# Adding the experts' rows to a running sum in DRAM, instead of keeping them and gathering them at the end

## What is computed

```python
scores = jax.nn.sigmoid(t @ w_router)                    # 512 tokens x 64 experts
# group-limited choice of 8 experts for each token, then
w = w / jnp.sum(w, -1, keepdims=True) * ROUTED_SCALE     # the token's 8 gates
h = silu(einsum('td,edf->tef', xb, w_gate)) * einsum('td,edf->tef', xb, w_up)
routed = einsum('tef,efd->td', h * gb[:, :, None], w_down)
shared = (silu(t @ ws_gate) * (t @ ws_up)) @ ws_down
x = layernorm(ALPHA * x + (1.0 + g2) * (routed + shared), ln2_g, ln2_b)
```

## Time and profile before

| | |
|---|---|
| median of 3 runs | 1363.83 us (1359.28 to 4515.15) |
| profiled execution: its time | 1363.99 us |
| its span, first to last instruction | 1362.2 us |
| mean granted clock of TensorE, share of full speed | 0.927 |
| PE, PEld, DVE, ACT, POOL busy | 87%, 66%, 56%, 26%, 11% |
| DMA read and written | 310.56 MB and 40.39 MB |

### The profile page before, as it was taken

How to read it: one execution, slowest core, us unless ns; L and a number is a source line. 1 busy time by engine, 2 the same in 40 slices (tenths; PEclk the granted TensorE clock), 3 DMA queues, 4 the chain that set the end, 5 groups by cost and what they waited for, 6 DMA issues and landing times.

```text
span 1362.2 us, 16041 instructions
## 1 busy us (share of the span) xinstructions
PE 1186.4 (87%) x5690; PEld 899.2 (66%) x5690; DVE 760.9 (56%) x1179; ACT 352.7 (26%) x533; POOL 149.2 (11%) x135
## 2 busy tenths in 40 slices
PE   2889997996989988779999999999999999999400
PEld 2443444655644577668888888888888888888300
DVE  4565698755224753665555555555555555555398
ACT  0222312225640021222222322222222222222100
POOL 0000000000000000440000000000000010000276
PEclk9787998997999999789999999999999999999755
DMA  9994253006100344569999999999999999995293
GB/s 352 327 338 160 78 81 104 1 4 231 75 1 16 123 171 156 211 228 325 362 352 356 349 355 352 352 350 351 360 344 356 352 355 349 358 354 206 94 374 134
DMA packets 77528, 333.56 MB, mean 245 GB/s; under 512 B 14601, under 2 KB 16521, under 8 KB 52537
## 3 DMA queue, kind: packets, MB, share of 16 engines
q1 hardware_dynamic: 58104, 291.05, 58.7%
q0 software_dynamic: 14112, 33.58, 6.8%
q10 hardware_dynamic: 5280, 8.53, 1.9%
HBM read 310.56 MB, written 40.39 MB: 258 GB/s over the span
## 4 chain that ended last, share of the span: by engine, by line
PE 72%; DVE 15%; DMA 7%; ACT 2%; issue 2%; SPq 2%; POOL 0%; ACTq 0%; POOLq 0%; DVEq 0%
PE ps L632 31%; PE ps L655 14%; PE ps L684 5%; PE ps L1481 4%; PE ps L1271 4%; DVE acc L922 3%; DMA xg<-u_rows,idx 3%; PE ps L1279 3%; DMA fk<-in_w_ada 3%; DVE big L1595 2%; PE ps L1345 2%; DVE small L1593 2%; DVE big L1527 2%; SPq L959 2%; PE ps L1451 1%
## 5 line engine op out<-in xcount | busy, mean ns | idle before, releaser
L632 PE MATMUL ps<-wx,xT 128*128 128x256 f32 x2048 | 452.8, 379 | 1.7 <-DVE xT L876 1.0
L632 PEld LDWEIGHTS ps<-wx,xT 128*128 128x128 f32 x2048 | 384.7, 190 | 51.6 <-issue 2.0
L751 DVE TENSOR_TENSOR wd_lo<-wx,wd_hi 128x2048 fp32r<-128x2048 f32 x65 | 149.0, 2292 | 40.8 <-ACT wd_hi L558 38.7
L558 ACT ACTIVATE wd_hi<-wx 128x2048 fp32r<-128x2048 f32 x64 | 122.3, 1911 | 143.5 <-PE ps L655 143.5
L504 POOL DMA_INDIRECT xg<-u_rows,idx x66 | 65.6, 994 | 667.3 <-DVE idx L867 667.0
L884 DVE TENSOR_TENSOR yrow<-ps,vg 128x512 f32<-128x512 f32 x64 | 44.3, 692 | 147.7 <-PE ps L655 147.7
L655 PE MATMUL ps<-wd_hi,hT_hi 128*128 128x512 f32 x272 | 116.5, 428 | 10.9 <-DVE hT_lo L756 9.5
L1271 PE MATMUL ps<-uT,ring 128*128 128x512 f32 x272 | 120.5, 603 | 0.0
L567 ACT ACTIVATE hs<-ps 128x256 f32<-128x256 f32 x68 | 26.1, 384 | 333.3 <-PE ps L632 333.3
L655 PE MATMUL ps<-wd_hi,hT_lo 128*128 128x512 f32 x272 | 111.6, 410 | 0.0
L745 DVE TENSOR_TENSOR hs<-hs,ps 128x256 f32<-128x256 f32 x68 | 28.6, 420 | 147.6 <-ACT hs L567 147.6
(11 more groups left out here) (268 smaller groups left out, 1376.3 us busy)
## 6 DMA issues: line engine op xcount, KB each, us to landing
wx<-in_w_gate SPq DMA_DIRECT2D x64, 1024.0 KB
wx<-in_w_up SPq DMA_DIRECT2D x64, 1024.0 KB
wx<-in_w_down SPq DMA_DIRECT2D x64, 1024.0 KB
expert_rows<-yrow SPq DMA_DIRECT2D x64, 512.0 KB
ring<-in_w_in SPq DMA_DIRECT2D x6, 2048.0 KB, 16.0
vg<-in_w_ada SPq DMA_DIRECT2D x4, 2048.0 KB, 9.1
fk<-in_w_ada SPq DMA_DIRECT2D x4, 2048.0 KB, 10.4
ring<-in_w_ada SPq DMA_DIRECT2D x3, 2048.0 KB, 13.7
```

The lines of the kernel that those rows point to most:

```text
L558: act.activation(wd_hi[:], flat_weights(s)[2], ACT.Copy).then_inc(wd_hi_ready, 1)
L632: mm = pe.matmul(ps[u % 2][:, k * ED:(k + 1) * ED], lhs(j), w[:, j, :], start=(j == 0), stop=(j == KD - 1))
L751: dve.tensor_tensor(wd_lo[s][:], w, wd_hi[:].bitcast(F32), ALU.subtract).then_inc(wd_ready, 1)
```

## The change

The gate is applied to an expert's row when the row leaves PSUM, and the row is added there and then to its token's row in a sum of 512 rows in DRAM (`expert_sums`), which is filled first with the shared expert's output. Part by part:

- The sum has 128 spare rows. An empty slot p of a list points to spare row 512 + p, so that each transfer has 128 different rows; for the gather these still lie beyond the bound.
- The gate of each slot comes out of the same one-hot matmuls: `tok_gate` holds for each token and expert the token number's high part and the gate in three bfloat16 pieces; 4 of the 8 small matmuls have 4 columns instead of 1, and `indices` adds the three pieces.
- `rows_out` moves from DVE to ACT, ahead of `weights_high`. It scales by the slot's gate.
- The store of SP is gone. In its place POOL issues after each gather an indirect transfer that adds the 128 rows of the step before to the sum (`add_rows`). It waits for `rows_out` and for the adding transfer before it to have landed (two lists can hold the same token). `indices` waits until the adding transfer of four lists earlier has landed, since `idx` has four columns.
- `cnt`, `base`, `akey`, `output_slots`, the 32 gathers, the 32 multiply-adds, ACT's and POOL's preparation of `acc` are gone. The end is: wait for the last adding transfer, four plain loads of the sum (512 KB each), and per tile one multiply by 1 + g2 and one multiply-add of ALPHA * x, then the layer norm as before.

The core of the diff:

```diff
--- before.py
+++ after.py
...
     with ExitStack() as ctx:
         def sb(name, shape, dt=F32, at=ctx):
...
             load(2, 2, (2,))
             load(3, 3, (0,))
+            sp.wait_ge(y2_left, VIRT)
+            sp.wait_ge(y2_right, VIRT)
+            for t in range(NT):
+                sp.dma_start(sum_d[t * P:(t + 1) * P, :], acc[:, t, :]).then_inc(sum_stored, 16)
             n_steps = steps(sp)
 
-            def store(u, row, waits, stored):
-
-                sp.wait_ge(y_stored, stored)
-                sp.wait_ge(y2_left, waits)
-                sp.wait_ge(y2_right, waits)
-                sp.dma_start(y_d[bass.ds(row, P), :], yb_[:, u % 2, :]).then_inc(y_stored, 16)
-
-            def first_row(col):
-                return sp.value_load(base_i[0:1, bass.ds(col, 1)], min_val=0, max_val=T * EK)
-
-            n16 = sp.snap(n_steps * 16)
             with sp.Fori(0, n_steps - UNROLL, UNROLL) as i:
-                i16 = sp.snap(i * 16)
                 for u in range(UNROLL):
                     done = sp.snap(i + (VIRT + u + 1))
-                    stored = sp.snap(i16 + (u + 4) * 16)
-                    row = first_row(i + u)
                     e = sp.snap((i + (UNROLL + u)) % NE)
 
                     sp.wait_ge(gu_done, done)
                     load(u, e, (0, 1))
                     sp.wait_ge(y2_done, done)
                     load(u, e, (2,))
-                    store(u, row, done, stored)
-            for u in range(UNROLL):
-                done = sp.snap(n_steps + (VIRT + u + 1 - UNROLL))
-                row = first_row(n_steps + (u - UNROLL))
-                stored = n16 + u * 16
-
-                done = sp.snap(sp.to_reg(done), min_val=1, max_val=1024)
-                store(u, row, done, stored)
+            sp.wait_ge(sum_stored, 16 * NT)
+            sp.wait_ge(y_added, 16 * n_steps)
+            for t in range(NT):
+                sp.dma_start(acc[:, t, :], sum_d[t * P:(t + 1) * P, :]).then_inc(sum_loaded[t], 16)
             for t in range(NT):
                 if t < NT - 1:
...
+            def add_rows(m, col):
+
+                pool.wait_ge(y2_left, m + (VIRT + 1))
+                pool.wait_ge(y2_right, m + (VIRT + 1))
+                if isinstance(m, int) and m == 0:
+                    pool.wait_ge(sum_stored, 16 * NT)
+                else:
+                    pool.wait_ge(y_added, 16 * m)
+                pool.reg_add(spare, zero, T + P - 1)
+                pool.indirect_dma_start(out=sum_d[:, :], out_offset=bass.IndirectOffsetOnAxis(ap=idx[:, col:col + 1], axis=0),
+                                        in_=yb_[:, col % 2, :], in_offset=None, bounds_check=spare, oob_is_err=True,
+                                        compute_op=ALU.add).then_inc(y_added, 16)
+
...
                 gather((u + 2) % 4, u % 2, last)
+                if not isinstance(i, int) or u >= 1:
+                    add_rows(i + (u - 1), (u - 1) % 4)
 
...
                 expert(0, u)
-
-                pool.wait_ge(y2_left, VIRT)
-                pool.wait_ge(y2_right, VIRT)
-                pool.wait_ge(x1_scaled, u + 1)
-                pool.tensor_tensor(acc[:, u, :], acc[:, u, :], mods[:, 3, :], ALU.mult).then_inc(sum_scaled, 1)
-                pool.wait_ge(sum_scaled, u + 1)
-                pool.tensor_tensor(acc[:, u, :], acc[:, u, :], x1[:, u, :], ALU.add).then_inc(sum_ready, 1)
             with pool.Fori(UNROLL, n_steps, UNROLL) as i:
                 for u in range(UNROLL):
                     expert(i, u)
-
-            pool.wait_ge(y_stored, 16 * n_steps + 64)
+            add_rows(n_steps - 1, UNROLL - 1)
             for b_ in range(2):
                 pool.wait_ge(gathered[b_], 8 * n_steps + 16)
-            for s in range(UNROLL):
-                pool.wait_ge(w_full[s], 12 * n_steps)
-            pool.reg_add(last, zero, T * EK - 1)
-            for t in range(NT):
-                if t >= YB:
-                    pool.wait_ge(yg_used, t - YB + 1)
-                for k in range(EK):
-                    pool.indirect_dma_start(out=yg[t % YB][:, k, :], out_offset=None, in_=y_d[0:T * EK, :],
-                                            in_offset=bass.IndirectOffsetOnAxis(ap=slot8i[:, t * EK + k:t * EK + k + 1], axis=0),
-                                            bounds_check=last, oob_is_err=False).then_inc(yg_loaded[t % YB][k], 16)
 
             pool.wait_ge(ln_loaded, 64)
             for t in range(NT - 1):
@@ -596,22 +570,33 @@
             act.activation(xT[:, 0, 0:4, :], ps[2][:].rearrange("p (j n) -> p j n", n=P), ACT.Copy).then_inc(xt2_act, 1)
             n_steps = steps(act)
 
+            def rows_out(i, u):
...
+
+                act.wait_ge(y2_done, i + (VIRT + u + 1))
+                if not isinstance(i, int) or u >= 2:
+                    act.wait_ge(y_added, 16 * i + (16 * u - 16))
+                gate = slot_gate[:, u % 4:u % 4 + 1]
+                act.activation(yb_[:, u % 2, 0:512], ps[6][:], ACT.Identity, scale=gate).then_inc(y2_left, 1)
+                act.activation(yb_[:, u % 2, 512:1024], ps[7][:], ACT.Identity, scale=gate).then_inc(y2_right, 1)
+
             def expert(i, u):
                 silu_gate(i + (VIRT + u), u)
                 act.wait_ge(xt2_done, i + (u + 2))
                 act.activation(xT[:, (u + 1) % 2, 0:4, :], ps[2][:].rearrange("p (j n) -> p j n", n=P),
                                ACT.Copy).then_inc(xt2_act, 1)
                 act.wait_ge(y2_done, i + (VIRT + u))
...
             with act.Fori(UNROLL, n_steps, UNROLL) as i:
                 for u in range(UNROLL):
                     expert(i, u)
+            rows_out(n_steps, -1)
 
             for t in range(NT):
                 act.wait_ge(r_ready, NT + t + 1)
@@ -672,9 +657,14 @@
                 pe.wait_ge(hot_ready, n + 1)
...
+                e = slice(n, n + 1) if isinstance(n, int) else bass.ds(pe.snap(n % NE), 1)
                 for t in range(NT):
-                    pe.matmul(ps[5][:, 0:1], sel1[:, k % 2, t, :], tok_hi[:, t:t + 1], start=(t == 0), stop=False)
-                    mm = pe.matmul(ps[5][:, 0:1], sel1[:, k % 2, t, :], tok_lo[:], start=False, stop=(t == NT - 1))
+                    if t >= 1:
+                        pe.matmul(ps[5][:, 0:1], sel1[:, k % 2, t, :], tok_lo[:], start=False, stop=False)
+                    mm = pe.matmul(ps[5][:, 0:4], sel1[:, k % 2, t, :], tok_gate[:, t, e, :].rearrange("p a b -> p (a b)"),
+                                   start=(t == 0), stop=(t == NT - 1))
+                    if t == 0:
+                        pe.matmul(ps[5][:, 0:1], sel1[:, k % 2, t, :], tok_lo[:], start=False, stop=False)
                 mm.then_inc(idx_done, 1)
...
+            dve.wait_ge(xg_zero, 4)
+            by_e = lambda a: a.rearrange("p (t e) -> p t e", e=NE)
+            seq(dve.tensor_copy(tok_gate[:, :, :, 1], gates[:]))
+            seq(dve.tensor_tensor(by_e(tmp), gates[:], tok_gate[:, :, :, 1], ALU.subtract))
+            seq(dve.tensor_copy(tok_gate[:, :, :, 2], by_e(tmp)))
+            seq(dve.tensor_tensor(by_e(tmp), by_e(tmp), tok_gate[:, :, :, 2], ALU.subtract))
+            seq(dve.tensor_copy(tok_gate[:, :, :, 3], by_e(tmp)))
+            turned_low(1, 1)
+            gate_times_up(2, 2)
...
-
-                for r in range(MAXPASS):
-                    step(dve.tensor_scalar(cnt[:, r, :], ps[3][:, 0:NE], float(-P * r), 0.0, ALU.add, ALU.max))
-                step.wait()
-                seq(dve.tensor_scalar(cnt[:], cnt[:], float(P), None, ALU.min))
-                flat = lambda a: a[:].rearrange("p r e -> p (r e)")
-                seq(dve.tensor_copy(grow[:], ones[:, 0:1].broadcast_to([P, MAXPASS * NE])))
-                seq(dve.tensor_tensor_scan(flat(base), grow[:], flat(cnt), 0.0, ALU.mult, ALU.add))
-                seq(dve.tensor_tensor(flat(base), flat(base), flat(cnt), ALU.subtract))
-                seq(dve.tensor_copy(base_i[:], base[0:1].rearrange("p r e -> p (r e)")))
-                turned_low(1, 1)
-                gate_times_up(2, 2)
-
-                e_rows = lambda a: a.unsqueeze(1).broadcast_to([P, NT, NE])
...
-                dve.tensor_scalar(nit[0:1, 0:1], grp[0:1, 41:42], float(NE), float(NE), ALU.mult, ALU.add).then_inc(route_ready, 1)
-
-            def output_slots(tiles):
-
-                for t in tiles:
-                    seq(dve.max(slot8[:, t, :], akey[:, t, :]))
-                    seq(dve.tensor_scalar(slot8i[:, t * EK:(t + 1) * EK], slot8[:, t, :], -1.0, None, ALU.add))
-                    hit = rt[:, 4:6, :].rearrange("p a n -> p (a n)").rearrange("p (k e) -> p k e", e=NE)
-                    seq(dve.tensor_tensor(hit, akey[:, t, :].unsqueeze(1).broadcast_to([P, EK, NE]),
-                                          slot8[:, t, :].unsqueeze(2).broadcast_to([P, EK, NE]), ALU.is_equal))
-                    seq(dve.tensor_tensor(hit, hit, gates[:, t, :].unsqueeze(1).broadcast_to([P, EK, NE]), ALU.mult))
```

(44 more changed lines are left out.)

47 lines of the change are left out of this document (12 added, 35 removed).

## The result

The changed kernel takes 1465.84 us, the kernel before 1363.71 us in the same runs: a ratio of 1.0758 (95% interval 1.0729 to 1.0788). It is slower by 7.6%, where I forecast 1314 us and a range up to 1405. One of the four executions of the kernel before took 4515.15 us, and the ratio leaves it out.

What follows compares the result with a forecast made beforehand. PE was taken to set the pace at 11.1 us a step, with DMA room of 1.6 us. 1362.2 - 2.5 - 27.5 + 12 + 1.2 - 33 = 1312.4, plus 1.8: 1314 us; range 1288 to 1405.

Steps and rivals of the forecast that it cites:

- the part on the adding transfer as a wait: Steps' waits on adding transfers: POOL's just at the limit, ACT's and DVE's with more room; +12 us in all.
- The serial additions set the pace: Rival: each transfer waits on POOL for the one before; 1391 us from a 12.2 us landing, 1500 at 14; chance 0.23.
- The landing: Adding transfer under load with two passes: 4.5 + 1.3 + 5 = 10.8 us, between 7 and 16.
- The gather's stalls: Gather needed 9.4 us after issue misses in some steps: 0.2 us on average, +12 us, between 0 and 1 a step.
- The addition as load: DMA engines: the adding transfer costs two passes, 2.5 us, as the old row must be fetched too.
- The room: DMA engines: 1.6 us free a step before; with additions 4.47 MB, 10.8 us at 415 GB/s, 0.3 under PE's period.
- the first rival: DMA has a ceiling at 354 GB/s: 12.6 us a step, 1361 us; chance 0.15, shared with three passes.
- ACT's 1.2 us and the wider matmuls: Each step: `rows_out` ahead of `weights_high` costs nothing, between 0 and 0.3 us; four columns in eight small matmuls nothing.
- Front, first steps, tail: Before the first step -2.5 us; first four steps -27.5; after the last `down` -33, between -25 and -42.

Runs made afterwards that it cites:

- eight_columns: The changed kernel with eight columns instead of four for `idx` and `slot_gate`, loops unrolled by eight: 1324.48 us, 0.9727 of the kernel before.
- skip_empty: The changed kernel with the adding transfer's bound at the last real row, so empty slots move nothing: 1462.85 us, 1.0739 of the kernel before.
- two-sum kernel: The changed kernel with eight columns and two sums in DRAM, one for even and one for odd lists: 1320.47 us, 0.9695 of the kernel before.
- two_skip: The changed kernel with eight columns, two sums in DRAM, and empty slots moving nothing: 1320.80 us, 0.9715 of the kernel before.
- no_transfers: The changed kernel without the 64 adding transfers and the waits for them: 1292.02 us.
- xt_first: The changed kernel, still four columns, with DVE's copy of its half of `xT` ahead of `indices`: 1543.89 us.
- two_light: The changed kernel with two sums and eight columns, and only half of w_up loaded from the fifth expert on: 1304.01 us.

## Why the prediction was wrong

- **The step that failed** stands in the part on the adding transfer as a wait: "DVE's `indices`, with its half of `xT` behind it, one that went out 17 us before." I had the two facts and put them together wrongly. List k+2's numbers are written in step k, and go into list k-2's column; `down(k-2)` ends as step k begins, so that transfer leaves 2.2 us into the step, 5.7 us before DVE is ready to write the numbers (905.69 and 911.4 above), not 17; 17 us is about the distance to the transfer of list k-3, one period earlier. With a landing of 10.6 us that is 4.9 us of waiting in this step, 3.9 us on average, and `eight_columns`, which took the wait away, has 141 us back.
- **The rival was there, its mechanism was not.** "The serial additions set the pace" named POOL's wait of one transfer for the one before, at landing plus 0.3 us, with 12.2 us as the point of decision. By its own sum it would have cost nothing at the measured 10.6 us; the outcome is in its range, by another cause. In the changed kernel that wait is hidden; the pace comes mostly from a longer ring through two DMAs, `indices` between them. A ring of 10.6 + 9.4 us plus some 7.5 us over two steps gives 13.8 us. With the row of the gather (6.9 to 9.1) and my own 10.8 us it would have come to 12.6 to 13.7 us beforehand, had I followed the reuse of each buffer around.
- **The landing was right by luck**: 10.8 us forecast, 10.6 measured. Its parts were 4.5 for a full transfer, 1.3 for the second pass and 5 for the load; the runs have 3.4, 2.8 and 4.4. The 5 us rest on a misread row: the gathers that land in 2.1 us in the last steps are not half empty but empty, those of lists 64 and 65; the last one with real rows lands after 4.2 us. From there to 6.9 the load adds 2.7 us, and the sum would have been 8.5. Halving the rows did not shorten it either (`skip_empty`).
- **The gather's stalls were sized too small.** I had 0.2 us a step, 12 us in all, for gathers that miss their 9.4 us of cover. In `eight_columns`, where no column's wait hides it, PE waits 0.43 us a step for them, and the period is 0.46 us over 11.12, 28 us in 62 steps.
- **The addition as load** was right: 2.8 us for 2.5. The room was sized too large: at 415 GB/s a step's 4.47 MB (the old rows counted too) needed 10.8 us, and the two-sum kernel, whose weights are late, runs at 11.39. That is 392 GB/s. But `two_skip` moves only some 3.95 MB a step and its weights are just as late at the same 11.39 us, 347 GB/s. So the first rival was right that the weights can become late, and wrong on the size (12.6 us a step); what limits them is no single rate in GB/s, and it stays open.
- **ACT's 1.2 us and the wider matmuls** cost nothing, as said (`no_transfers`, 11.12 us).
- **Front, first steps, tail**: -2.55 us for -2.5, which is partly luck: `eight_columns`, `skip_empty` and `xt_first`, the same up to that point, start the first step at 529.19, 528.51 and 530.76 instead of 532.25. 11.12 us from the second step on once no wait is in the way. -37 for -33, with POOL beside DVE as described; but POOL ends before DVE and is not on the chain, where I had it.
- With eight columns the forecast of 1314 us would have been 0.8% too low, in a kernel that I had not forecast.

## What to carry to other kernels

A buffer's depth is a wait. When a change lets a slow reader (here a DMA of 10 us) hold on to a small buffer, count the time from the reader's start to the next writer's turn in the timeline of one step, list by list, and then walk the ring from that writer back to the reader: its length over its number of steps is a floor for the period that no row of busy time shows. Two DMAs in one ring of two steps left PE, DVE and the DMA engines all below full, which is what such a ring looks like in the windows; and four more columns turned 7.6% slower into 2.7% faster. Then read the chain again: the eight-column kernel was held by the next ring, through the gather alone.

## What the runs showed of the hardware

- An indirect transfer of 128 rows of 4 KB lands in 3.4 us unloaded and 10.0 loaded; with addition 6.2 and 10.6; with addition and half of its rows beyond the bound 6.1 and 11.1. Under load neither the rows moved nor the addition make up most of it.
- POOL's issue of an adding transfer takes 1.59 us, of a plain one 1.03 us. Where it starts while DVE's `wd_lo` runs (918.66 above, DVE since 918.47) it takes up to 3.6 us: all 21 such issues of the changed kernel end 1.46 or 1.47 us after `wd_lo` does. The other order costs nothing: in 37 steps `wd_lo` starts 0.2 to 1.0 us into POOL's issue, and takes its 2.29 us as ever. The Trainium skill (SBUF — State Buffer, section "SBUF: two separate sides") has a DVE operation with two inputs in SBUF and a GpSimd operation that reads SBUF share a port pair, which whoever starts first holds for its whole instruction while the other waits. The 21 issues agree with that; the 37, where DVE came second and did not wait, do not.
- w_down landed 15 us later after its issue (22.4 for 7.4) while the mean share of the DMA engines was 0.9 (`two_skip`), and in 7.1 us with 0.5 MB less of weights a step (`two_light`). Which engine or which of the queue's turns is full there was not tried.
